# Layer norms as two fused VectorE operations, on top of re-ordered chunk steps and re-tiled decode rows, in a two-layer hybrid decoder

## What is computed

```python
def reference(x_prompt, x_sample, ...):
    for l in range(DEPTH):                      # 2
        m, ... = _mix_prompt(xp, w_in[l], w_out[l], ...)
        xp = _post_block(xp, m, ...)
        m, ... = _mix_sample(xs, state_ret[l], state_hgrn[l], cache_swa_k[l], cache_swa_v[l], ...)
        xs = _post_block(xs, m, ...)
def _post_block(x, mix, g1, b1, w_up, w_down, g2, b2):
    x = _layernorm(ALPHA * x + mix, g1, b1)
    h = relu(x @ w_up)                          # 1024 -> 4096
    return _layernorm(ALPHA * x + (h * h) @ w_down, g2, b2)
def _layernorm(x, g, b):
    return (x - mean) * rsqrt(var + LN_EPS) * g + b
```

## Time and profile before

| | |
|---|---|
| median of 3 runs | 2952.43 us (2949.02 to 2953.35) |
| the profiled execution's own time | 2947.27 us |
| its span in the trace | 2945.5 us |
| mean granted TensorE clock | 0.951 |
| busy: PE, DVE, POOL, ACT | 91%, 46%, 33%, 30% |
| instructions | 42963 |

### The profile page before, as it was taken

The page is one execution under the profiler, slowest core; times in us unless marked ns, Lnnn a source line. Parts: engine busy times, 40 slices in busy tenths (PEclk is TensorE's granted clock), DMA queues, the critical chain, the costliest instruction groups (busy, mean ns, idle before and its releaser), DMA issues. The chain is left out here.

```text
span 2945.5 us, 42963 instructions
## 1 busy us (share of the span) xinstructions
PE 2685.7 (91%) x17494; PEld 2447.7 (83%) x17494; DVE 1357.1 (46%) x3012; ACT 876.1 (30%) x1724; POOL 958.2 (33%) x954
## 2 busy tenths in 40 slices
PE   6998888778999999999999888778799999999996
PEld 6997776577899999999899877656788999999996
DVE  2135567545443443434641365664454343343437
ACT  2235545313212111121232444551231212112122
POOL 0026555624212211112330464654332121111225
PEclk9999989789999999999999999897799999999998
DMA  4442222143211111110244431320521111111112
GB/s 151 141 148 78 82 91 54 38 119 124 67 44 44 53 49 44 44 44 29 97 152 143 135 97 50 95 64 17 181 84 58 44 44 49 52 44 43 44 36 104
DMA packets 182356, 226.43 MB, mean 77 GB/s; under 512 B 26256, under 2 KB 158672, under 8 KB 182128
## 3 DMA queue, kind: packets, MB, share of 16 engines
q1 hardware_dynamic: 182160, 223.70, 23.7%
HBM read 182.63 MB, written 43.06 MB: 77 GB/s over the span
## 5 line engine op out<-in xcount | busy, mean ns | idle before, releaser
L945 PE MATMUL ps<-u_hi,wu_hi 128*128 128x512 f32 (+2 forms) x1536 | 499.2, 325 | 0.0
L946 PE MATMUL ps<-u_lo,wu_hi 128*128 128x512 f32 (+2 forms) x1536 | 498.5, 325 | 0.0
L947 PE MATMUL ps<-u_hi,wu_lo 128*128 128x512 f32 (+2 forms) x1536 | 496.5, 323 | 0.0
L945 PE MATMUL ps<-hid_hi,wd_hi 128*128 128x256 f32 (+2 forms) x1472 | 473.9, 322 | 8.0 <-DVE acc_a L2391 3.6
L946 PE MATMUL ps<-hid_lo,wd_hi 128*128 128x256 f32 (+2 forms) x1472 | 472.3, 321 | 0.0
L947 PE MATMUL ps<-hid_hi,wd_lo 128*128 128x256 f32 (+2 forms) x1472 | 470.8, 320 | 0.0
L2359 DVE TENSOR_TENSOR relu<-relu 128x512 f32<-128x512 f32 (+2 forms) x192 | 108.7, 566 | 532.2 <-ACT relu L1844 531.8
L2655 POOL TENSOR_TENSOR wu_lo<-wu_raw,wu_hi 128x2048 fp32r<-128x2048 f32 x32 | 147.7, 4617 | 564.6 <-ACT wu_hi L1807 540.0
L945 PEld LDWEIGHTS ps<-u_hi,wu_hi 128*128 128x128 f32 x1536 | 290.1, 189 | 23.0
L947 PEld LDWEIGHTS ps<-u_hi,wu_lo 128*128 128x128 f32 x1536 | 290.9, 189 | 22.0
L946 PEld LDWEIGHTS ps<-u_lo,wu_hi 128*128 128x128 f32 x1536 | 290.2, 189 | 22.4
(11 more groups left out here) (268 smaller groups left out, 5517.5 us busy)
## 6 DMA issues: line engine op xcount, KB each, us to landing
wu_raw<-in_w_up SPq DMA_DIRECT2D x32, 1024.0 KB, 5.3
wd_raw<-in_w_down SPq DMA_DIRECT2D x32, 1024.0 KB, 4.8
wl_raw<-in_w_in SPq DMA_DIRECT2D x20, 1024.0 KB, 5.3
wi_raw<-in_w_in SPq DMA_DIRECT2D x15, 1280.0 KB, 6.9
out_y<-xn SPq DMA_DIRECT2D x32, 512.0 KB, 2.7
hscr<-h_out SPq DMA_DIRECT2D x80, 160.0 KB, 1.8
hb<-hscr SPq DMA_DIRECT2D x16, 512.0 KB, 4.3
xin<-out_y SPq DMA_DIRECT2D x16, 512.0 KB, 3.8
```

The lines of the kernel that those rows point to most:

```text
L945: nc.tensor.matmul(out, a_hi, b_hi, start=start, stop=False)
L946: nc.tensor.matmul(out, a_hi, b_lo, start=False, stop=False)
L947: return nc.tensor.matmul(out, a_lo, b_hi, start=False, stop=stop)
```

## The change

**Norms.** DVE does the affine part in two operations with a tile of 128x1024 each: (xin - mean) x ln_g, ahead of its wait for ACT's rstd, and (that) x rstd + ln_b behind the Newton step. `nmr`, ACT's `normed` and POOL's `scale` are gone. The waits for the store of tile t-2 and for PE's transposes of tile t-2 now stand on DVE. In attend_out, SP issues each of the first four stores of xn one or more loads earlier. `split_wi(l, 1)` on DVE stands ahead of `norm(7)`.

**Chunk steps.** The late unit of place b stands at c in steps 0 to 3, and the two of a2 at c in step 4. `gates` is cut in two on ACT and DVE: `gates_sigmoid` where it was, the logarithm and the gates' activations (`gates_log`) behind dense d, `window_high`, dense e and `heads_high`; on DVE `gates_clip` behind `window_low`. The high part of weight group 8 is made one late unit earlier (`HIGH_AT`). `last_rows()` stands at the front of step 7.

**Decode rows.** The states are read into a bank of their own, four column groups of 32 rows at a time (64 products), ACT copies that bank to `parts`, and one product with a constant (`sum4`) adds the groups up. The `kdm` products stand ahead of it. DVE adds the retention states first (`decode_states_r`, ahead of `heads_moments`), the gated states last (`decode_states_h`). The window's output takes 16 products with 32 stationary columns and 128 moving ones, an ACT copy and two transposes.

```diff
-PLACES = {(-1, "p"): 3, (-1, "q"): 2, (0, "a1"): 3, (0, "a2"): 2, (0, "b"): 1, (0, "c"): 1, (0, "d"): 2, (0, "e"): 1}
-PLACES |= {(s, x): n for s in (1, 2, 3) for x, n in (("a1", 2), ("a2", 2), ("b", 1), ("c", 1), ("d", 1))}
-PLACES |= {(4, "a1"): 2, (4, "a2"): 2}
+PLACES = {(-1, "p"): 3, (-1, "q"): 2, (0, "a1"): 3, (0, "a2"): 2, (0, "c"): 2, (0, "d"): 2, (0, "e"): 1}
+PLACES |= {(s, x): n for s in (1, 2, 3) for x, n in (("a1", 2), ("a2", 2), ("c", 2), ("d", 1))}
+PLACES |= {(4, "a1"): 2, (4, "c"): 2}
+HIGH_AT = {LATE * (G - 1) + 1 - (G == 8): G for G in range(2, GROUPS_B)}
@@ SP load_x, store_y
-                    sp.wait_ge(nx.sem, nx.at("xn", n - 2))
+                    sp.wait_ge(nq.sem, nq.at("g", n - 2))
-                sp.wait_ge(npl.sem, npl.at("b", n))
+                sp.wait_ge(nq.sem, nq.at("b", n))
@@ SP mix step
+                    if s == 7:
+                        last_rows()
                     dense(s, "a1")
...
-                    if s == 7:
-                        last_rows()
@@ SP attend_out
                 load_x(l, 0, 2)
+                store_y(l, 0, 0)
                 load_wo(l, 13)
...
                 load_x(l, 0, 3)
-                store_y(l, 0, 0)
+                store_y(l, 0, 1)
                 load_wo(l, 14)
                 load_x(l, 0, 4)
-                store_y(l, 0, 1)
+                store_y(l, 0, 2)
@@ PE decode_window
-                    for b in range(NB):
-                        r = slice(32 * (b % 4), 32 * (b % 4) + 32)
-                        nc.tensor.matmul(ps[:, 5, 32 * b:32 * b + 32], cv[:, b, :], spT[:, b // 4, r],
-                                         start=True, stop=False)
...
+                    for i in range(2):
+                        to = slice(P * i, P * i + P)
+                        for e in range(4):
+                            r = slice(32 * e, 32 * e + 32)
+                            nc.tensor.matmul(ps[r, 5, to], spT[:, i, r], cv[:, 4 * i + e, :], start=True, stop=False)
...
+                    last.then_inc(dpe.step("w"), 1)
+                    pe.wait_ge(da.sem, da.at("w", l))
+                    for i in range(2):
+                        last = transpose(ps[:, 4, i * P:(i + 1) * P], s_prob[:, i, 0:P], P)
@@ PE decode_heads_out
+                    for h in range(4):
                         for b in range(NB):
+                            r = slice(32 * (b % 4), 32 * (b % 4) + 32)
+                            nc.tensor.matmul(ps[r, 1, 64 * h:64 * h + 64], qm_r[:, h, b, :], s0_r[:, b, :],
+                                             start=(b < 4), stop=(b >= 4))
...
+                    pe.wait_ge(da.sem, da.at("parts", l))
+                    nc.tensor.matmul(ps[0:rows, 0, :], cst("sum4"), parts[:], start=True, stop=False)
@@ ACT
-            def normed(l, which, t):
...
-                nc.scalar.activation(xn[p][rs], xin[which][p][rs], ACT.Identity, bias=nmr[rs, p:p + 1], scale=rstd[rs, p:p + 1])\
-                    .then_inc(nx.step("xn"), 1)
@@ ACT mix_step
                         if g:
-                            gates(g)
+                            gates_sigmoid(g)
                         dense(step, "d")
                         window_high(f)
...
                     dense(step, "e")
+                    if h:
+                        heads_high(h)
+                    if f and f.prompt and g:
+                        gates_log(g)
@@ DVE norm
+                if t == 0:
+                    dve.wait_ge(ln_in, 32 * (2 * l + which + 1))
+                if n >= 2:
+                    before = y_stores(l, which, t) - 16
+                    dve.wait_ge(y_out[p], before)
+                if t >= 2 and (l + 1 < DEPTH or not which):
+                    dve.wait_ge(spe.sem, spe.at("T", split_no(l, which, t - 2)))
+                v.scalar_tensor_tensor(out=xn[p][rs], in0=xin[which][p][rs], scalar=aggr[rs, p, 0:1], in1=ln_g[rs],
+                                       op0=ALU.subtract, op1=ALU.mult).then_inc(nq.step("g"), 1)
                 dve.wait_ge(na.sem, na.at("r", n))
                 newton(rstd[rs, p:p + 1], var[rs, p:p + 1], newt[rs, p:p + 1], dve, nq, n)
                 dve.wait_ge(nq.sem, nq.at("rstd", n))
-                v.scalar_tensor_tensor(out=nmr[rs, p:p + 1], in0=aggr[rs, p, 0:1], scalar=-1.0, in1=rstd[rs, p:p + 1],
-                                       op0=ALU.mult, op1=ALU.mult).then_inc(nq.step("nm"), 1)
+                v.scalar_tensor_tensor(out=xn[p][rs], in0=xn[p][rs], scalar=rstd[rs, p:p + 1], in1=ln_b[rs],
+                                       op0=ALU.mult, op1=ALU.add).then_inc(nq.step("b"), 1)
@@ DVE mix_step
                         if g:
-                            gates(g, h)
+                            gates_sigmoid(g)
                         window_low(f)
+                        if g:
+                            gates_clip(g, h)
@@ POOL
-            def scale(l, which, t):
...
-                g_.tensor_tensor(xn[p][rs], xn[p][rs], ln_g[rs], ALU.mult).then_inc(npl.step("g"), 1)
-                pool.wait_ge(npl.sem, npl.at("g", n))
-                g_.tensor_tensor(xn[p][rs], xn[p][rs], ln_b[rs], ALU.add).then_inc(npl.step("b"), 1)
```

More of the change, by code:

```diff
@@ L792, in step @@
                     if s == 4:
+                        next_v(5)
+                        dense(s, "c")
                         late_rows()
@@ L799, in step @@
                                          A[src][bass.ds(l, 1), :, NL:WIN, :]).then_inc(cache_out, 16)
-                    if s == 7:
-                        last_rows()
-                    if s and s + 1 < TILES:
+                    if s and s != 4 and s + 1 < TILES:
                         next_v(s + 1)
-                    for place in "bcde":
-                        dense(s, place)
+                    if s != 4:
+                        for place in "bcde":
+                            dense(s, place)
                 def last_rows():
@@ L1621, in mix, with gates_sigmoid @@
             def mix(l):
-                def gates(c):
+                def gates_sigmoid(c):
                     act.wait_ge(gc.sem, gc.at("clip", c.n))
@@ L1660, in heads_square @@
                     rows = c.rows
+                    if not c.prompt:
+                        act.wait_ge(dpe.sem, dpe.at("parts", l))
+                        copy(parts[:], ps[:, 1, :]).then_inc(da.step("parts"), 1)
                     act.wait_ge(mpe.sem, mpe.at("o", c.n))
@@ L1713, in decode_window @@
                         .then_inc(da.step("T"), 1)
+                    act.wait_ge(dpe.sem, dpe.at("w", l))
+                    copy(s_prob[:, :, 0:P], ps[:, 5, 0:256].rearrange("p (a b) -> p a b", a=2)).then_inc(da.step("w"), 1)
                     act.wait_ge(dpe.sem, dpe.at("o", l))
@@ L2224, in heads_merge, with heads_states @@
                         .then_inc(md.step("sr"), 1)
+                    if c.prompt:
+                        heads_states(c)
+                    dve.wait_ge(md.sem, md.at("sr", c.n))
+                    v.tensor_tensor(cat_h[0:rows, :], ps[0:rows, 0, :], gate[c.p][0:rows]
+                                    .rearrange("p a b -> p (a b)"), ALU.mult).then_inc(md.step("rh"), 1)
+                def heads_states(c):
                     dve.wait_ge(mpe.sem, mpe.at("st", c.n))
@@ L2254, in heads_merge @@
-                    dve.wait_ge(md.sem, md.at("sr", c.n))
-                    v.tensor_tensor(cat_h[0:rows, :], ps[0:rows, 0, :], gate[c.p][0:rows]
-                                    .rearrange("p a b -> p (a b)"), ALU.mult).then_inc(md.step("rh"), 1)
+                        a = 256 + pr * P + 64 * j
+                        v.scalar_tensor_tensor(out=st_h[d, pr, d], in0=st_h[d, pr, d],
+                                               scalar=g_eb[c.p][d, pr, P - 1:P],
+                                               in1=ps[d, 2, a:a + 64], op0=ALU.mult, op1=ALU.add)\
+                            .then_inc(sdv.step(f"h{h}"), 1)
@@ new lines, in decode_states_h @@
+                def decode_states_h(c):
+                    dve.wait_ge(dd.sem, dd.at("hm", l))
+                    dve.wait_ge(mpe.sem, mpe.at("st", c.n))
+                    for h in range(4):
+                        pr, j = h // 2, h % 2
+                        d = slice(64 * j, 64 * j + 64)
+                        add = ps[d, 4 + 2 * pr:6 + 2 * pr, :].rearrange("p b (e c) -> p (b e) c", e=4)[:, :, d]
+                        v.tensor_tensor(s0_h[d, pr], s0_h[d, pr], add, ALU.add)\
+                            .then_inc(dd.step(f"h{h}"), 1)
@@ L2310, in mix_step @@
                         decode_masks(f)
+                    if h and not h.prompt:
+                        decode_states_r(h)
                     if h:
@@ L2663, in _ @@
             for l in range(DEPTH):
-                if l:
-                    for t in range(6, TILES):
-                        scale(l - 1, 1, t)
                 split_late(l, 0)
@@ L2670, in _ @@
                 barrier(pool, 2 * l + 2)
```

(8 more changed lines are left out.)

188 lines of the change are left out of this document (83 added, 105 removed).

## The result

| | before | after |
|---|---|---|
| median | 2952.89 us (2949.02 to 2955.75, 4 runs) | 2869.41 us (2867.16 to 2874.48, 4 runs) |
| ratio to before | | 0.9721, 95% interval 0.9703 to 0.9738 |
| profiled span | 2945.5 us | 2864.9 us |
| mean granted clock | 0.951 | 0.962 |

What follows compares the result with a forecast made beforehand. PE, busy 2685.7 of 2945.5 us, bounded the kernel, so gain came from its idle time or the clock. 2 x (-47.6 - 12 - 12.5) + 12 = -132 off the median gave 2820 us, range 2775 to 2885.

Steps and rivals of the forecast that it cites:

- the clock: Chunk steps: of some 62 us at 0.50 behind waits, 12 per layer come back, bounds 0 and 25; 1 in attend_out.
- new waits on ScalarE: Chunk steps: PE comes sooner to ACT's copies of the next front and w_out's first high part; +3.8 us per layer.
- the signs named ahead: L1117's and prob's waits below 15 us, chunk steps 345 to 365, attend_out near 65, new operations 1.2, decode window 3.2.
- the first rival: Chunk steps: PE waits for ACT's chain after window_high, only half of 59.6 us per layer; 2880, 0.26 with units without effect.
- that on the level products: Chunk steps: with window_high and window_low earlier, PE's wait shrinks by 20.2 us per layer, twice 40 of 50.0.
- The slower case: Norms: DVE's queue stands behind the store of tile t-2, up to 7.14 us for 28 tiles; 3020, chance 0.06.
- The moved units: Chunk steps, rival: moving late units does nothing, DVE binding the window's chain; 35 us less gain, 2855; within the 0.26.
- The third rival: Decode rows: four column groups run abreast, state reads and window take a quarter; 8 us per layer, 2804, chance 0.06.
- the decode rows' term: Decode rows, per layer: the window products' new form gains 6.5 us, the reordered adds in step 9 net 3.6.
- The bound of 1.92: Norms: DVE's new operations, stretched by POOL's work, take 1.92 us instead of 1.22; 20 us more in all.

Runs made afterwards that it cites:

- e3: The norms' part of the change alone (with its order of stores in attend_out), on the kernel before: 2933.3 us, ratio 0.9935.
- e10: e1 with the norms' part undone (norms and order of stores as in the kernel before): 2858.39 us, ratio 0.9678.
- e5: The decode rows' part of the change alone, on the kernel before: 2930.11 us, ratio 0.9924.
- e6: e1 with the late unit of place c back at b in steps 0 to 3: 2863.98 us, ratio 0.9699.
- e8: e1 with ScalarE's gates in one piece again, ahead of window_high: 2881.59 us, ratio 0.9764.
- e7: e1 with last_rows() back behind the loads for dense a1 and a2 in step 7: 2846.41 us, ratio 0.9647.
- e11: e1 with the high part of weight group 8 made where it was before: 2843.67 us, ratio 0.9633.
- e1: The changed kernel with VectorE's gates_clip ahead of window_low again ("the version with the clips first"): 2835.63 us, ratio 0.9606.
- e2: The changed kernel with g_q and g_k, in step 4 alone, behind the window's and the heads' casts: 2871.74 us, ratio 0.9726.
- e9: The changed kernel, order kept, with the gates' clip written as a scalar_tensor_tensor in place of the tensor_scalar: 2876.65 us, ratio 0.9734.
- e4: The changed kernel with the retention state reads in the order 0, 4, 1, 5, 2, 6, 3, 7: one execution, 2865.74 us.

## Why the prediction was right, and where it fell short

The direction and the range held, and so did the mechanisms of most parts. The table goes part by part. The forecasts leave the clock out, which was priced apart (24 us); the measured differences have it in:

| part | forecast | measured |
|---|---|---|
| norms | -13 | -19 alone (e3), -21 on top (e10) |
| decode rows | -20 | -22 alone (e5) |
| late unit from b to c, steps 0 to 3 | -24 | -27 (e6) |
| gates cut on ScalarE | -23 | -47 (e8) |
| `last_rows()` at the front | -17 | -12 (e7) |
| group 8 earlier | -7 | -8, not clear of noise (e11) |
| two units of step 4 from a2 to c | -11 | not run alone |
| new waits on ScalarE | +8 | not run alone |
| clips behind `window_low` | not priced | +34 (e1) |

The parts do not simply add up: taken away one by one from e1's version, or added alone, they make 135 us, and that version is 116 us faster than the kernel before.

Of the signs named ahead, those of the norms came: attend_out took 67 and 70 us, and the new operations 1.28. Those of the chunk steps did not: L1122 waits 57 us, not below 15, `prob` 21.7, not below 15, and the chunk steps fell by 30 to 34 us per layer and not by 60. The measured time is nearer to the first rival's 2880 than to 2820, and it is inside the range because the range was made to take that rival in.

**The step that failed** is that on the level products: "the last obstacle is DVE: its gates end where ACT's logarithm starts, at 1903.7, and `window_low` takes 0.7". It priced the move of `window_low` ahead of the clips, and left the clips' new place at nothing, without naming what ran beside it. Just ahead of that place stands ScalarE's cast of the late weights, whose end releases GpSimd's split. The move put two short operations of VectorE under a 4.5 us operation of GpSimd in steps 0 to 2 of both layers. e1 shows this to be 34 us. With it away the kernel stands at 0.9606, 116 us below before, against 132 forecast.

**What remains** is above all step 4. I took 2.9 us off its wait per layer (3.7 in both layers before), and in the changed kernel it is 6.3 and 6.7. Moving two late units behind scores B made PE come sooner to what GpSimd's chain ends, and that chain starts with the landing of loads. That is the first rival, "the freed steps run into the next late thing", though at GpSimd and not, as I put it, at ScalarE's copies of the front. That the moved units are the reason is read from the traces and was not run alone. e2 shows that one other order on ScalarE and VectorE doesn't help. An order with `g_kt` ahead of `g_k`, and an earlier start of GpSimd's chain, weren't tried.

**The clock.** I took 26 us back, 12 per layer in the chunk steps and 1 in attend_out. What came back can be estimated from PE's busy time: it fell by 37.5 us in the changed kernel, of which the decode rows alone make 19 (2685.7 to 2666.4 in e5, at the mean clock of before). That leaves some 18 us, with 218 us at 1.2 GHz (2864.9 x 0.038 x 2) against 289. The version with the clips first was busy another 6 us less, which makes some 25, with 187 us at 1.2 GHz. Waits of over 4 us stayed in steps 1, 2 and 4 of each layer of the changed kernel. My half-way value could not know which.

**The rivals.** The slower case, VectorE's queue behind the stores of xn, fell outright: 0.7 us of such waits in the whole run, where it needed 4.7 per tile. The first tile waits for ln_b instead, 11.2 us in both layers together. The moved units did their work (e6). The third rival, column tiles side by side, which I gave 0.06, fits what was seen in the state reads. I had read L1160 against L1187 at 0.07 us a pass each, and overlooked two things: a pass of L1160 has 128 moving columns and one of L1187 has 64, and L1160 ran at a granted clock of 0.50 (421 ns for one pass) and L1187 at 1.00 (220 ns). Per column and at the same clock L1160, in four column groups, was already four times as fast, and it writes to two banks, so the row spoke for the groups. In layer 1 the window's 32 passes took 2.6 us, against 2.2 priced, and the state reads 2.2 us where 8.6 had been taken as unchanged. So the decode rows' term is right in part by luck: by an estimate from the durations in e5, some 10 of its 22 us are the state reads', which were not priced, and the priced parts brought some 12 of 20. The gain was spent in part, since the decode rows' window weights wait longer (from 1.7 to 4.5 us, for `s_prob`).

**Contention of the new norm operations.** The bound of 1.92 wasn't met: 1.28 us each everywhere. It wasn't put to the test either: of the 72 new operations only two began while an operation of GpSimd ran, 0.1 us ahead of its end. The same pair of engines collided elsewhere, in both forms tried: 0.28 against 3.68 us, and 0.41 against 3.81 (e1, e9). The Trainium skill ("GPSIMD Engine Reference", Specifications) names instructions in a two-port mode and those with two inputs from SBUF as the ones that collide; e9, with two inputs, agrees.

## What to carry to other kernels

When an operation is moved on one engine, look at what the other engines run at the new place, not only at what it waits for and who waits for it: two operations of 0.3 us, six times under a neighbour's 4.5 us, cost 34 us of run time. A wait that shrinks can be met again behind the next producer, so take the next late one from the trace before you count the gain. And compare passes per column and at the same granted clock before you say that two shapes cost the same, or that an order changed their time.

## What the runs showed of the hardware

- 64 passes with 32 stationary and 64 moving columns took 1.1 us when they were spread over four column groups, and 4.3 with all in one group, both at a granted clock of 1.00. At 0.50 the spread ones took 1.93 us, and 1.96 with neighbours paired in one group (e4). The Trainium skill ("TensorEngine Tiling (Array Packing)", Key Properties) says that different tiles can load and multiply in parallel; the fall from 4.3 to 1.1 agrees.
- An operation of VectorE that reads and writes SBUF, begun beside GpSimd's split of 128x2048, ended only with it (3.62 us, and 3.68 at most, for one that takes 0.28 alone). Two forms of it, with one input and with two, did the same (e9). One that reads PSUM and SBUF was not slowed (0.69).
